# The attention's input product with seven products per quarter, x streamed from DRAM

## Time and profile before

| what | us |
|---|---|
| median of 3 runs (2003.45 to 2006.34) | 2005.15 |
| the profiled execution | 2001.48 |
| its span, first to last instruction | 1999.6 |
| TensorE busy | 1914.5 |
| VectorE, ScalarE, GpSimd busy | 1161.7, 701.3, 431.5 |
| preparation, projection, attention, pool stage (about) | 133, 558, 321, 987 |

### The profile page before, as it was taken

The page is one execution under the profiler, slowest core; times in us unless marked ns, Lnnn a source line. Parts: engine busy times, 40 slices in busy tenths (PEclk is TensorE's granted clock), DMA queues, the critical chain, the costliest instruction groups (busy, mean ns, idle before and its releaser), DMA issues.

```text
span 1999.6 us, 24456 instructions
## 1 busy us (share of the span) xinstructions
PE 1914.5 (96%) x8974; PEld 1588.5 (79%) x8974; DVE 1161.7 (58%) x1539; ACT 701.3 (35%) x1065; POOL 431.5 (22%) x268
## 2 busy tenths in 40 slices
PE   8999999999999989999949999999999999999997
PEld 7778887888888778888738888887888886787786
DVE  4330102332415277787675688868678657546998
ACT  4441213131313243343354444344434335224331
POOL 0005200000000000000043666423334343322430
PEclk9999999999999999999979999999999999999999
DMA  8766530334233464455322444333322225647342
GB/s 254 221 202 239 178 103 17 108 87 118 79 101 87 159 242 164 172 187 170 136 96 74 153 141 152 135 104 137 129 88 73 94 74 193 249 170 272 129 177 95
DMA packets 229912, 287.74 MB, mean 144 GB/s; under 512 B 17216, under 2 KB 170176, under 8 KB 227904
## 3 DMA queue, kind: packets, MB, share of 16 engines
q1 hardware_dynamic: 225216, 278.20, 42.0%
q10 hardware_dynamic: 4608, 8.39, 1.1%
HBM read 186.93 MB, written 99.61 MB: 143 GB/s over the span
## 4 chain that ended last, share of the span: by engine, by line
PE 41%; DVE 4%; issue 4%; ACT 1%; POOL 0%; DVEq 0%; POOLq 0%; ACTq 0%
PE banks L165 13%; PE banks L166 13%; PE banks L167 13%; DVE m_w_lo L1922 1%; DVE m_x_lo L1936 1%; ACT m_x_hi L1728 0%; DVE m_x_lo L1914 0%; PE banks L1621 0%; PE banks L1668 0%; DVE m_stats L2025 0%; DVE m_x_lo L1896 0%; DVE m_res L2019 0%; DVE m_res L2035 0%; POOL m_s L1859 0%; DVE m_win_b L1968 0%
## 5 line engine op out<-in xcount | busy, mean ns | idle before, releaser
L165 PE MATMUL banks<-m_x_hi,m_w_hi 128*128 128x512 f32 x1320 | 517.6, 392 | 9.4 <-DVE m_res L2019 3.5
L166 PE MATMUL banks<-m_x_lo,m_w_hi 128*128 128x512 f32 x1320 | 515.3, 390 | 0.0
L167 PE MATMUL banks<-m_x_hi,m_w_lo 128*128 128x512 f32 x1320 | 515.0, 390 | 0.0
L165 PEld LDWEIGHTS banks<-m_x_hi,m_w_hi 128*128 128x128 f32 x1320 | 248.7, 188 | 63.7 <-DVE m_w_lo L1922 10.0
L166 PEld LDWEIGHTS banks<-m_x_lo,m_w_hi 128*128 128x128 f32 x1320 | 248.8, 188 | 52.0 <-issue 0.7
L167 PEld LDWEIGHTS banks<-m_x_hi,m_w_lo 128*128 128x128 f32 x1320 | 248.7, 188 | 52.0
L1854 POOL TENSOR_TENSOR m_s<-pair_raw 128x512 f32<-128x512 f32 x24 | 47.3, 1969 | 891.6 <-POOLq L947 757.5
L165 PE MATMUL banks<-x_hi,h_w_hi 128*128 128x512 f32 x512 | 199.9, 390 | 0.8 <-DVE h_g_out L833 0.8
L166 PE MATMUL banks<-x_lo,h_w_hi 128*128 128x512 f32 x512 | 199.3, 389 | 0.0
L167 PE MATMUL banks<-x_hi,h_w_lo 128*128 128x512 f32 x512 | 199.3, 389 | 0.0
L1716 ACT ACTIVATE m_w_hi<-m_s 128x512 fp32r<-128x512 f32 x184 | 115.5, 629 | 202.7 <-PE banks L167 179.2
(11 more groups left out here) (220 smaller groups left out, 3117.7 us busy)
## 6 DMA issues: line engine op xcount, KB each, us to landing
p_in<-in_pool_w_in SPq DMA_DIRECT2D x32, 256.0 KB, 4.9
p_rows<-in_x SPq DMA_DIRECT2D x16, 512.0 KB, 5.2
w_fused<-p_out SPq DMA_DIRECT2D x32, 256.0 KB, 3.9
h_out_rows<-in_pool_w_out SPq DMA_DIRECT2D x16, 512.0 KB, 6.7
v_tiles<-v_out ACTq DMA_DIRECT2D x32, 256.0 KB, 2.1
w_terms<-h_out_terms SPq DMA_DIRECT2D x8, 1024.0 KB, 5.6
h_raw<-in_gla_w_in SPq DMA_DIRECT2D x16, 512.0 KB, 4.2
g_tiles<-h_g_out SPq DMA_DIRECT2D x32, 256.0 KB, 2.3
```

What stands on the lines that cost most here:

```text
L165: nc.tensor.matmul(out, a_hi, b_hi, start=first, stop=False, skip_group_check=True)
L166: nc.tensor.matmul(out, a_hi, b_lo, start=False, stop=False, skip_group_check=True)
L167: return nc.tensor.matmul(out, a_lo, b_hi, start=False, stop=last, skip_group_check=True)
```

## The change

Both halves of the projection become 24 steps of one form, the form of the pool stage (Winograd's variant of Strassen's scheme). A step takes a 2 x 2 arrangement of weights (four blocks of 4 x 128 rows by 128 columns) and a 2 x 2 arrangement of moving operands (blocks of 4 x 128 rows by 512 columns), and does seven products of 4 x 3 matmuls in place of eight. The products come in the order j = 1, 5, 6, 2, 7, 3, 4. Four sums of weights (s1 to s4) are made by GpSimd; the moving side has seven blocks b_raw[j], split into b_hi[j] and b_lo[j], of which four are differences.

- Steps 0 to 7 do the values. The moving side is the value weights, made ready in `prepare`; the stationary side is a pair of row tiles of x, turned, read back from a new DRAM scratch `x_in`. In each of these steps VectorE makes four differences for `w_terms` (out_terms, in slots 1 and 2) and four of the pair of x (x_terms, slots 4 and 5), through one buffer `terms`.
- Steps 8 to 15 and 16 to 23 do the heads for each half of the rows. The moving side is x, as seven blocks of 1 MB, loaded from `x_in` at i = 7 and i = 15 and split on ScalarE (`turn_hi`) and VectorE (`turn_lo`). They are read as four pieces of 128 columns, 2 KB apart. One step does q and k of a head, or the two g columns of a head; the order of the eight units and the slots of the decays' work are tables.
- In `prepare`, x is stored to `x_in` instead of kept; four 1 MB value loads come at n = 10, 12, 14 and 16; GpSimd makes 16 differences of them; ScalarE and VectorE split the seven blocks at n = 18, 20, ..., 30, after `b_summed` has reached 16. `load_first_pair` comes at n = 24.
- `w_fused` is stored as plain rows (2 KB pieces where it were 512 B), and the pool stage reads it in pieces of 512 B.
- The last stores of keys and gates and the ten loads of `load_qkv` come after the last step's work.

The core of the diff:

```diff
+    V_LOADS_AT = {10: 1, 12: 7, 14: 3, 16: 2}
+    V_PARTS_AT = {n: j for n, j in zip(range(18, 32, 2), ORDER)}
+    PAIR_AT = 24
...
+                def store_x(t):
+                    sp.wait_ge(x_copied, t + 1)
+                    half, c, b = t // KT, t % KT // 2, t % 2
+                    sp.dma_start(p.x_in[half, 2 * b:2 * b + 2, :, c, :].rearrange("q p n -> p q n"),
+                                 x_out[t % 2][:].rearrange("p (q k) t -> p q (k t)", q=2)
+                                 ).then_inc(p.x_in_stored[t % 2], DMA)
...
                     if n >= 2:
                         store(n - 2)
+                    if x_tile(n) is not None and x_tile(n) >= 1:
+                        store_x(x_tile(n) - 1)
+                    if n in V_LOADS_AT:
+                        load_values(V_LOADS_AT[n])
+                    if n == PAIR_AT:
+                        load_first_pair()
...
+                for j in V_LOADS:
+                    pool.wait_ge(b_loaded[j], DMA)
+                for k in range(HALF_K):
...
                     if n >= 1:
                         copy_out(n - 1)
+                    if n in V_PARTS_AT:
+                        act.wait_ge(b_summed, 4 * HALF_K)
+                        j = V_PARTS_AT[n]
+                        nc.scalar.activation(p.b_hi[j][:], p.b_raw[j][:], ACT.Copy).then_inc(b_hi_done, 1)
```

In `project`, SP:

```diff
+            for i in range(STEPS):
+                e = i // EPOCH + 1
+                for n in range(-1, PRODUCTS - 1):
+                    if n == -1 and 1 <= i <= V_STEPS:
+                        store_v(i - 1, 1)
+                    if n == -1 and i and i % EPOCH == 0:
+                        load_x(e - 1, PRODUCTS - 1)
+                    if n >= 0 and i % EPOCH == EPOCH - 1 and i + 1 < STEPS:
+                        if n == 0:
+                            sp.wait_ge(terms_stored, 2 * HALF_K * e * DMA)
+                        load_x(e, n)
+                    if i < V_STEPS:
+                        if n == 3:
+                            store_out_terms(i)
+                            if i + 1 < 2 * HALF_K:
+                                load_out_rows(i + 1)
+                        elif n == 5:
+                            sp.wait_ge(x_summed, 4 * (i + 1))
+                            load_pair(i + 2)
+                            store_v(i, 0)
+                            store_x_terms(i)
...
+            store_kn(2 * HEADS - 1)
+            store_gates(2 * HEADS - 1)
...
+            for s in range(2):
+                p.load_qkv(sp, s, s)
```

TensorE and ScalarE in a step:

```diff
+            def product(i, n):
+                j = ORDER[n]
+                pe.wait_ge(w_lo_done, PRODUCTS * i + n + 1)
+                if i and i % EPOCH == 0:
+                    pe.wait_ge(x_lo_done, turns_to(i // EPOCH, n))
...
+                for k in range(HALF_K):
+                    last = split_product(nc, shaped(i, bank(i, j)), w_hi[j][:, k, :], w_lo[j][:, k, :],
+                                         moving(i, x_hi[j], k), moving(i, x_lo[j], k), opens and k == 0, k == HALF_K - 1)
...
+                    elif n == 0:
+                        seed(i)
+                    elif n == 2:
+                        copy_u2(i)
+                    elif n == 3:
+                        copy_p5(i)
+                        if i < V_STEPS:
+                            copy_c11(i)
+                    for turn in turning(TURN_HI, i, n):
+                        turn_hi(*turn)
+                    if n >= 0:
+                        hi_part(i + 1, n)
```

`free(i, j)` lets product 7 (j = 4) of a step wait for `u3_added`, product 5 (j = 7) for `u2_copied`, product 6 (j = 3) for `p5_copied`; `hi_part(i + 1, n)` waits for the pair's load or GpSimd's sum and for product n of step i. VectorE in a step:

```diff
+            def x_terms(i, part):
...
+                if part == 0:
+                    dve.wait_ge(terms_stored, (2 * i + 1) * DMA)
...
+                    elif n == 4:
+                        add_u3(i)
+                    elif n == 5:
+                        add_c12(i)
+                    for turn in turning(TURN_LO, i, n):
+                        turn_lo(*turn)
+                    if n >= 0:
+                        lo_part(i + 1, n)
...
+                    if i < V_STEPS:
+                        if n in (1, 2):
+                            out_terms(i, n - 1)
+                        elif n in (4, 5):
+                            x_terms(i, n - 4)
```

More of the change, by code:

```diff
@@ L182, in prepare @@
     t_lo = [p.place(f"p_t_lo{s}", [P, GT, P], F32R) for s in range(2)]
-    out = [p.place(f"p_out{s}", [P, GW]) for s in range(2)]
-    rows = [p.place(f"p_rows{s}", [P, D]) for s in range(ROWS)]
+    assert p.at <= SBUF_END
     with ExitStack():
@@ new lines, in project @@
+    NORM_AT = {0: (1, 1), 1: (2, 3), 2: (5, 1), 3: (9, -1)}
+    TURN_HI = {0: (0, 3), 1: (0, 4), 2: (0, 5), 3: (1, -1), 4: (1, 0), 5: (1, 1), 6: (1, 2)}
+    TURN_LO = {0: (0, 4), 1: (0, 5), 2: (1, -1), 3: (1, 0), 4: (1, 1), 5: (1, 2), 6: (1, 3)}
+    x_hi, x_lo, x_raw = p.b_hi, p.b_lo, p.b_raw
+    p.at = p.in_end
+    raws = [p.in_raw0, p.place("h_raw1", [P, 2 * KT, P])]
+    s1, s2, s3, s4 = (p.place(f"h_s{n}", [P, HALF_K, P]) for n in range(1, 5))
+    assert p.at == p.qkv_at
+    e_q, e_k, sums = (p.place(f"h_{n}", [P, HALF]) for n in ("e_q", "e_k", "sums"))
@@ new lines, in project, with sem @@
+    assert p.at <= SBUF_END
+    p.at = p.qkv_at
+    rank_w = p.place("h_rank_w", [P, KT, RANK_ROWS], F32R)
+    p.at = p.qkv_at
+    v_out = [p.place(f"h_v_out{s}", [P, 2, D]) for s in range(2)]
+    assert p.at == alt_at
+    g_alt = p.place("h_g_alt", [P, 4, BLK])
+    p.at = alt_at
+    terms = p.place("h_terms", [P, 4, BLK])
+    p.at = g_at
+    out_rows = p.place("h_out_rows", [P, 2, D])
+    held = []
+    def sem(name):
+        held.append(nc.alloc_semaphore("h_" + name))
+        return held[-1]
@@ L472, in _, with gates, gate_stores, turns_to @@
+    def gates(m):
+        return g_alt if m % HEADS == 0 else g_main
+    def gate_stores(m, which):
+        return sum((o % HEADS == 0) == (which == ALT) for o in range(m)) * 4 * DMA
+    def turns_to(e, n):
+        return PRODUCTS * (e - 1) + n + 1
+    gk_ps = p.ps[:, 6:8, :].rearrange("p b t -> p (b t)")
+    CHAINED = 5
+    with nc.Block() as block:
         @block.sync
         def _(sp):
-            def load(h, j):
-                sp.dma_start(raw[j % 2][:], w_src[:, :, ds(w_cols(h, j), P)]).then_inc(loaded[j % 2], DMA)
@@ new lines, in rank_rows @@
+            def rank_rows(i):
+                half = i // EPOCH - 1
+                pe.wait_ge(rank_lo, 3 * (half + 1))
+                if half:
+                    pe.wait_ge(kn_copied, 2 * HEADS * half)
+                for n, parts in enumerate((((1, 0), (2, HALF_K)), ((1, 0), (5, 0), (3, HALF_K)))):
+                    count = 0
+                    for j, first in parts:
+                        for k in range(HALF_K):
+                            for x in (x_hi[j], x_lo[j]):
+                                count += 1
+                                last = nc.tensor.matmul(shaped(i, p.ps[0:RANK_ROWS, 6 + n, :]), rank_w[:, first + k, :],
+                                                        moving(i, x, k), start=count == 1,
+                                                        stop=count == len(parts) * 2 * HALF_K)
+                    last.then_inc(rank_mm, 1)
@@ L859, in attend_and_norm @@
+            norm_of(2 * HEADS - 1)
+    for s in held:
+        nc.gpsimd.sem_clear(s)
+        nc.release_semaphore(s)
 def attend_and_norm(nc, p, a):
```

1026 lines of the change are left out of this document (616 added, 410 removed).

## The result

The changed kernel takes 2071.86 us in the median (2004.89 for the kernel before on the same chip): ratio 1.0339, interval 1.0324 to 1.0353. One of its four runs, at 2418.31 us with a granted clock of 0.742 instead of 0.965, is left out of the ratio; the median of the other three is 2071.18. The kernel is slower by 67 us, where I forecast 25 and a range up to 2058. The profiled execution has 2069.3 us and a span of 2067.6; before it was 2001.5 and 1999.6.

What follows compares the result with a forecast made beforehand. The projection was taken as bound by TensorE's matmul count, the preparation as looser. Savings of 61.7 and 5 us against added waits summed to +25.3 us, so 2030 us from 2005.15, range 1994 to 2058.

Steps and rivals of the forecast that it cites:

- products and rank: Projection: 288 fewer matmuls save 65.3 us, the gate-rank product's extra matmuls cost 3.6; net -61.7 us.
- preparation: Before the projection: waits for GpSimd's 16 subtractions, late splits on ScalarE and VectorE, fuller DMA; +22 us (12 to 30).
- value steps: Steps 0 to 7: store and load waits through buffer terms make a step 23.5 us against 19.0; +28 us.
- first turn: Steps 7 and 8: x's seven loads and their splits come late and hold product 6; +18 us (6 to 25).
- second turn: From i = 15: VectorE's splits and keys crowd its slots, the seventh load queues behind stores; +8 us (4 to 14).
- Silu: Head steps: a Silu unit with its table load in slot 2 delays copy_p5 by 1.2 us, twice; +2 us.
- start and what is left of the projection: Projection's start: the ramp behind the first products goes, with other small waits; -5 us (0 to -10).
- end: Between last product and attention: keys, Silus, gate stores and ten load issues all follow the last product; +14 us (10 to 18).
- pool stage and attention: After the projection: pool-stage pair loads in 512 B pieces, loaded two steps ahead, cost 0 (0 to +3).
- Rival A: Value steps: the chain through terms fits into a 19.0 us step, so the kernel is faster, 1992 us; chance 0.20.
- Rival C: Value steps: VectorE and GpSimd hold each other up, 2.5 us more per chain, 2060 us; chance 0.11.
- Rival D: Head steps: matmuls reading four separated pieces run at 0.25 us instead of 0.2267, 2061 us; chance 0.05.

Runs made afterwards that it cites:

- the three together: Changed kernel with values' weights loaded earlier, x's terms formed before output terms in value steps, second gate unit's Silu behind ScalarE's copy: 2016.54 us, ratio 1.0064.

## Why the prediction was wrong

The sign, the places and the end were right; the sizes were not, and nearly all of them erred to the same side. The price of each is taken over 19.04 us a step, or over the run without turns.

| step of the sum | forecast | measured |
|---|---|---|
| products and rank | -61.7 | -61.7: unhindered steps take 19.04 |
| preparation | +22 | +29.8 |
| value steps | +28 | +33.2 (seeds 0 to 7) |
| first turn | +18 | +22.7 |
| second turn | +8 | +9.4 |
| Silu | +2 | +8.8 |
| start and what is left of the projection | -5 | +11.1 |
| gap behind the preparation | 0 | +0.4 |
| end | +14 | +14.4 |
| pool stage and attention | 0 | -0.1 |

- **The step that failed most is "The start is a little better ... I take -5 (bounds 0 and -10)"**, with the small waits counted in: +11.1 in its place, 16 of the 43 us that the sum is short. Both halves of it were wrong.
  - The ramp at the start was never worth 5. I took the 4.0 us for `v_lo` in the earlier trace rows as waits behind the gap. They are the gap's 2.97 and two waits of 0.27 and 0.73:

```profile
140.44 0.50 PE L165 MATMUL banks<-v_hi,x_hi 128*128 128x512 f32 x1 [0.27 <-DVE v_lo L753]
...
142.81 0.50 PE L165 MATMUL banks<-v_hi,x_hi 128*128 128x512 f32 x1 [0.73 <-DVE v_lo L753]
```

  - From 135.29 to 142.81 the kernel before does 18 matmuls and loses 3.4 us against 0.2267 each. The kernel after does the 85 of step 0 from 165.46 to 187.62 and loses 2.9. So the start gained 0.5. (Seed 0 is no measure of it, since it stands behind ScalarE's roundings; it makes the value steps' row 1.4 too small and this one 1.4 too large.)
  - The head steps brought new waits, which the sum had at nothing or less. In the run without turns TensorE waits 11.5 us from step 8 on, where the kernel before has 2.4 behind its value products (1.6 for VectorE's `h_rank`, 0.8 for `h_g_out`): 9 of the 11.1. They are transposes behind VectorE's keys, products behind VectorE's sum `add_u3`, and 1.0 for a copy of ScalarE (who waited for whom: us in total, times, the longest):

```profile
PE banks L818 <- DVE h_sums L1220: 5.8, 5, 2.0
PE banks L173 <- DVE h_g_main L1084: 4.7, 3, 1.6
```

- **The preparation** had its wait for the sums nearly as worked out (9.8 us on ScalarE against 11.4, 14.05 on TensorE against 15.4), the sums took 20.6 us as said, and the earlier loads took 9 us away (10.9 in the trace). What I called "3 us more, of which 2 come back" did not come back: copy_out(17) was 8.3 us late before the wait began. A pair of tiles with a rounding took 8.44 us against 7.3, so 1.15 and not 0.85.
- **The value steps**: the step is 24.8 us, not 23.5. The step from 252.11 to 276.90 divides like the sum: output terms 5.0 (4.0 forecast), their store 5.7 (5.8), x's terms 3.8 (4.6), and from there to the next output terms 10.2 (9.1). The chain is not the one that I summed alone. I saw the pair's late load and called it "inside the same 23.5"; the run with the store first shows that it is a chain of its own which ended last, and the run with swapped terms that neither chain sets the step when the pair is loaded half a step earlier. Rival A's 19 us exist, but in an order that the change does not have. With the store first, the pair issued behind a 1 MB store took 2.5 us longer from its issue to its use. By the Trainium skill, "DMA: Bandwidth & Descriptors", section "Queues, rings and completion order", each DMA engine takes its descriptors in ring order; the trace agrees (8.8 us from issue to use instead of 6.3).
- **The turns** were near. TensorE's longest wait of the projection, 6.64 us, stands in step 8 as foreseen. I had the seventh load as the late one; its rounding came at 386.86, 34.9 us after the last output terms began (38 forecast), with 2.4 us of TensorE behind it. But ScalarE waited for earlier parts too (2.93, 0.68 and 2.82 us), so a part of the agreement in the sum is luck. In the second turn the order of the keys and of their store held 3.8 us, which I had not named.
- **Silu**: I counted 1.2 us for the late copy; it was 2.65 twice with a slow stretch of TensorE behind, since both table loads and three Silus stand ahead of the copy.
- **The end** was right in its steps: the Silus were done 5.2 us after the last product (5.7 forecast), the gates' stores were issued at 8.3 (8.4), the ten loads at 14.6 (13.9), and v had landed at 16.6 (16).
- **Rival C** came in part: beside GpSimd's weight sums the first two output terms of each step take 1.4 and 1.8 us instead of 0.69, and that is the 1.0 us by which the chain's first piece is too long; the rival had 2.5. With the swapped terms VectorE's `w_lo` still take up to 1.78 beside GpSimd, and the step is 19.04, so there they set nothing. The Trainium skill, "SBUF — State Buffer", section "SBUF: two separate sides", has one of the two engines blocked for the other's whole instruction; the lengthened operations agree with it. **Rival D** is refuted: the head steps 10 and 18 read the four pieces and take 19.04 us once the Silu is out of the way.

The stalls also cost TensorE's clock: the granted clock over the projection's two stretches was 0.93 and 0.97, where the earlier trace rows has 0.99 and 1.00. I priced stalls by the wait alone; in value steps 1 to 6 the slow matmuls cost 12.3 us beside 22.3 of waits.

## What to carry to other kernels

Where a step gets its input from a load that its own engines release, write down each chain that closes over a step, not the one through the obvious buffer, and load the next input as early in the step as its buffer allows; here one reordering gave back 30 us of 67. A saving in products that turns resident operands into streamed ones has to be charged for the stretches in which the queue is full: five other orders of the same work bought none of it back here. Add the stalls' slower clock and the small waits to such a sum, since here they all had one sign. And before a wait is counted as gone, look whether its total already holds a gap that is counted elsewhere.

## What was not expected of the hardware

- In the kernel after, four loads of parameter columns held SyncE for 0.45, 1.59, 2.75 and 4.87 us, the last from 78.58 to 83.45, and all stores behind them waited. The same four took 0.43, 0.51, 0.48 and 1.69 us in the kernel before, where the DMA share of that stretch is 0.75 instead of 1.05:

```profile
75.78 2.75 SPq L293 DMA_DIRECT2D b_grp<-in_pool_b_grp  x1
78.58 4.87 SPq L293 DMA_DIRECT2D scale<-in_pool_scale  x1
```

- A pair load from the weights took SyncE 13.53 us to issue while x's parts were under way (first row, the run with the pair's load moved), and 0.99 us in a quiet stretch (second row, the three together). That it is the full queue which holds the issuing engine is inferred from the two stretches:

```profile
309.22 13.53 SPq L623 DMA_DIRECT2D h_raw<-in_gla_w_in  x2
```
```profile
362.36 0.99 SPq L623 DMA_DIRECT2D h_raw<-in_gla_w_in  x2
```
